# Seven-product steps in four chunk pairs of the second up product

## The chip, the cores and the metric

The kernel runs on one core of one Trainium2 chip. The metric is the device time of one execution in microseconds (us). Engines: TensorE (PE, its weight loads PEld), VectorE (DVE), ScalarE (ACT), GpSimd (POOL) and SyncE (SP).

## The reference

Two transformer-like blocks in float32 on 256 tokens of width 2048. The part that the change touches is the gated feed-forward product of the second block:

```
h = rmsnorm_2(x, g_ffn)                       # 256 x 2048
u = causal_dwconv(h @ w_up, ffn_conv_w) + ffn_conv_b   # w_up 2048 x 11264, conv of width 3 over tokens
gate, val = split(u, 2)
x = x + (silu(gate) * val) @ w_down
```

## The kernel before

**Numbers.** Every float32 operand is split in two fp32r numbers, hi and lo. A product is three matmuls, hi by hi, hi by lo and lo by hi. The activations are TensorE's weights (128x128), the weight matrix streams through as 128x512.

**Granules.** A weight matrix arrives in granules of 128x1024: two k tiles of 512 columns. SP loads a granule into one of four raw slots (L868), once the granule four before it has been split. ScalarE casts it to `wh` (L937), VectorE makes the remainder `wl` (L1293), TensorE multiplies it with `multiply_half` (L1868): two k tiles, two halves of the tokens, three matmuls, 12 in all. `wh` and `wl` have four slots (RING), so a cast waits until TensorE has left the granule four before it (L936). A chunk is 512 output columns, here 8 granules, and sums into two PSUM banks.

**Order.** Everything is planned in steps, one a granule: in step s granule s is cast and split, granule s-3 is multiplied, and small work is put down at chosen steps with `later`. Within a step stand first the granule, then the small work in the order in which it was put down. Each engine then goes through its part of the plan strictly in this order, and waits at semaphores in front of each operation. So an operation whose input is late holds up all that stands behind it on its engine.

**The second up product** (`w_up2`, operand `ffn2`, tiles `x4g`): 22 chunks. The first two are interleaved, the others follow each other. What follows a chunk that ends at granule L is planned by `plan_up` from s = L + 4: `up_rows` (ScalarE, PSUM to ST, L1215) at s, `turn` (VectorE transposes ST into Y, L1410, L1412) and `leave` (POOL stores Y to HBM, L1816) at s+1, `bring` (POOL loads it back, rearranged, into Z, four transfers, L1824) at s+3, `up_keep` (ScalarE, Z to FW, L1223) at s+9, then the convolution's taps: `up_first` at s+10 (ScalarE, four, L1231), `up_second` at s+11 (VectorE, four, L1740), `up_third` at s+12 (VectorE, four, L1747, L1750), `up_silu` at s+13 (ScalarE, L1235), `up_gated` (VectorE, L1754) and `act2_hi` (ScalarE, L1239) at s+14, `act2_lo` (VectorE, L1758) at s+15.

**The seven-product step** is there already in the gated stage (the up product of the first block, ten pairs of chunks) and in both down products. Two chunks of a pair are multiplied side by side. For chosen rows p of the weight (a row is two k tiles) the two granules of row p, one of each chunk, are taken together as a 2x2 product of blocks (two halves of tokens or k by two chunks) and computed with seven block products of three matmuls, 21 instead of 24. For it VectorE adds weight blocks (`sums`, three operations, L1321, L1324, L1326), ScalarE casts three blocks (`base_hi`, L957) and the four sums (`forms_hi`, L963), VectorE makes the remainders (`base_lo`, L1307; `forms_lo`, L1330). TensorE multiplies in two parts, `multiply_base` (9 matmuls) and `multiply_forms` (12). Four of the products gather in four shared PSUM banks. Five steps behind a pair's last such row `shared_out` copies them out (ScalarE, four, L979), then `shared_sums` (L1366, L1368), `shared_last` (L1373, L1375) and per chunk `shared_bank` (L1396, L1397, L1401) add them up and into the chunks' own banks on VectorE. Once a stage the sums of activation blocks are made (`xs_sum`, `xs_hi`, `xs_lo`). Fetches of a step's successor four granules on wait for its `base_lo`.

Of the kernel before, what the change touches and what calls it, by code (L numbers as in the profile page):

```python
# [8 lines left out]
P = 128  # L9
# [11 lines left out]
ALU = mybir.AluOpType  # L21
ACT = mybir.ActivationFunctionType
F32 = mybir.dt.float32
# [74 lines left out]
def two_block_kernel(nc, t, out):  # L98
    with ExitStack() as ctx:
# [10 lines left out]
        def view(name, shape, offset, dt=F32):  # L110
            return nc.alloc_sbuf_tensor_at(name, shape, dt, offset=offset)
# [115 lines left out]
        tile_sums = tmp.rearrange("p (k c) -> p k c", k=4)  # L227
# [4 lines left out]
        xs_in, gated_in = (view(n, [P, 2, 4, P], o) for n, o in (("xs_in", o_a), ("gated_in", o_b + 32 * K)))  # L232
        xs_out, gated_out = (view(n, [P, 2, 4, P], o) for n, o in (("xs_out", o_a + 4 * K), ("gated_out", o_b + 36 * K)))
# [44 lines left out]
        seven_operand = {"gated": "ffn", "out1": "act1", "down": "act2"}  # L278
        side_by_side = {"gated": {}, "out1": {}, "down": {}}
# [68 lines left out]
        def turn(step, src, filled):  # L348
# [133 lines left out]
        def plan_gated(n):  # L482
            def after(s, chunk):
                chunk.drained = [("silu", n), ("gated", n)]
                if n // 2 in GATED_PAIRS:
                    do("shared_bank", n)
# [12 lines left out]
            return after  # L499
# [178 lines left out]
        for n in range(2, 22):  # L678
            last_up = product(t["w_up2"], "N", "ffn2", PAIRS16, ("up", n), plan_up(n), n)
# [79 lines left out]
        def gated_at(n):  # L759

            return at("shared_bank", n) if n // 2 in GATED_PAIRS else product_of("gated", n)
# [54 lines left out]
        bases = {"gated": (gated_hi, gated_lo), "out1": (base_hi, base_lo), "down": (base_hi, base_lo)}  # L816
        x_places = {"gated": (gated_in, gated_out), "out1": (xs_in, xs_out), "down": (xs_in, xs_out)}
# [4 lines left out]
        def x_forms(unit):  # L822

            if unit.pair.stage == "gated":
                return [[x[:, unit.place, n] for x in (gated_xs_hi, gated_xs_lo)] for n in range(4)]
            k = 2 * unit.p
            return [[x[:, k, P:T] for x in operands[seven_operand[unit.pair.stage]]]] + [
                [x[:, unit.place, n] for x in (xs_hi, xs_lo)] for n in range(3)]
# [87 lines left out]
        def scalar(e):  # L916
# [8 lines left out]
            for name, args in phases:  # L925
# [32 lines left out]
                elif name == "forms_hi":  # L958
# [3 lines left out]
                    e.wait_ge(*at("sums", i))  # L962
                    e.copy(two_slots(wh, i), tile_sums.rearrange("p k c -> p (k c)")).then_inc(done[name], 1)  # L963
                elif name == "xs_hi":
                    stage, j = args
                    e.wait_ge(*at("xs_sum", stage, j))
                    if stage == "gated":
                        e.copy(gated_xs_hi[:], gated_out[:]).then_inc(done[name], 1)
                        continue
                    e.copy(seven_tiles(operands[seven_operand[stage]][0], stage, j)[:, :, 1], xs_out[:, :, 0])  # L970
                    e.copy(xs_hi[:, 2 * j:2 * j + 2], xs_out[:, :, 1:4]).then_inc(done[name], 1)
                elif name == "shared_out":
# [5 lines left out]
                    for k, place in enumerate((0, 3, 2, 1)):  # L978
                        e.copy(tile_sums[:, place, :], ps[:, pair.shared + k, :]).then_inc(done[name], 1)  # L979
# [228 lines left out]
                elif name == "up_rows":  # L1208
# [5 lines left out]
                    e.wait_ge(*product_of("up", n))  # L1214
# [49 lines left out]
        def vector(e):  # L1264
# [22 lines left out]
            for name, args in phases:  # L1287
# [20 lines left out]
                elif name == "sums":  # L1308
                    i, = args
                    unit = seven[i]  # L1310
                    b12, b11, b22, b21 = (two_slots(raw, i)[:, 512 * k:512 * k + 512] for k in range(4))
                    if unit is not unit.pair.units[0]:
                        e.wait_ge(*at("forms_lo", unit.former.i))
                    else:
# [12 lines left out]
                elif name == "forms_lo":  # L1327
                    i, = args
                    e.wait_ge(*at("forms_hi", i))
                    e.tensor_tensor(two_slots(wl, i), tile_sums.rearrange("p k c -> p (k c)"), two_slots(wh, i).bitcast(F32),  # L1330
                                    ALU.subtract).then_inc(done[name], 1)
                elif name == "xs_sum":
# [3 lines left out]
                    if j > 0:  # L1336
                        e.wait_ge(*at("xs_lo", stage, j - 1))
                    elif stage != "gated":

                        e.wait_ge(*through(last_ffn if stage == "out1" else last_up))  # L1340
# [9 lines left out]
                elif name == "xs_lo":  # L1350
                    stage, j = args
                    e.wait_ge(*at("xs_hi", stage, j))
                    if stage == "gated":
                        e.tensor_tensor(gated_xs_lo[:], gated_out[:], gated_xs_hi[:].bitcast(F32),
                                        ALU.subtract).then_inc(done[name], 1)
                        continue
                    hi, lo = (seven_tiles(x, stage, j)[:, :, 1] for x in operands[seven_operand[stage]])
# [3 lines left out]
                elif name == "shared_sums":  # L1361

                    stage, q = args
                    p1, p7, p6, _ = (tile_sums[:, k, :] for k in range(4))
# [4 lines left out]
                elif name == "shared_last":  # L1369
                    stage, q = args  # L1370
                    _, second, first, p5 = (tile_sums[:, k, :] for k in range(4))
# [4 lines left out]
                elif name == "shared_first":  # L1376
# [5 lines left out]
                    e.tensor_tensor(X[:, 0, n0], X[:, 0, n0], tile_sums[:, 0, :], ALU.add)  # L1382
                    e.tensor_tensor(X[:, 1, n0], X[:, 1, n0], tile_sums[:, 1, :], ALU.subtract).then_inc(done[name], 1)
                elif name == "shared_second":
# [4 lines left out]
                    e.tensor_tensor(X[:, :, n1], X[:, :, n1], tile_sums[:, 2:4, :], ALU.add).then_inc(done[name], 1)  # L1389
                elif name == "shared_bank":  # L1390
                    n, = args
                    bank0, bank1 = banks(named["gated", n])
                    e.wait_ge(*product_of("gated", n))
                    if n % 2 == 0:
                        e.wait_ge(*at("shared_sums", "gated", n // 2))
                        e.tensor_tensor(bank0, bank0, tile_sums[:, 0, :], ALU.add)  # L1396
                        e.tensor_tensor(bank1, bank1, tile_sums[:, 1, :], ALU.subtract).then_inc(done[name], 1)  # L1397
                    else:
                        b = named["gated", n].bank
                        e.wait_ge(*at("shared_last", "gated", n // 2))  # L1400
                        e.tensor_tensor(ps[:, b:b + 2, :], ps[:, b:b + 2, :], tile_sums[:, 2:4, :], ALU.add).then_inc(done[name], 1)  # L1401
# [774 lines left out]
```

## Time and profile before

| | us |
|---|---|
| median of 3 runs (2407.12 to 2408.91) | 2408.24 |
| the profiled execution | 2406.19 |
| its span | 2404.4 |
| TensorE busy | 2391.4 (99%) |
| VectorE busy | 1748.8 (73%) |
| ScalarE busy | 1351.3 (56%) |

Busy time is the sum of an engine's operations. Matmuls are pipelined: each lasts 0.389 us in the records and they start closer than that, so a busy share of 99% says only that one or another was always under way. The second up product lies between 1686.24 and 2164.96 us from the span's start.

### The profile page before, as it was taken

The numbers are of one execution on the slowest core, as the hardware profiler recorded it, in microseconds if no ns is written. First come the engines' busy times: TensorE is split into PE (matmuls) and PEld (weight loads), VectorE is DVE, ScalarE is ACT, GpSimd is POOL, SyncE is SP. The second block draws the span as 40 slices with busy tenths as digits, with TensorE's granted clock in tenths as the row PEclk, the third lists the DMA queues.
The fourth block names the chain that finished last, engine by engine and source line by source line (L and its number), as shares of the span: only waits on it lengthen the run. The fifth ranks groups of instructions, "written<-read, shape, count | busy, mean of one in ns | idle before, by whom it ended". The sixth has DMA issues, their size and how long they took to land.

```text
span 2404.4 us, 28031 instructions
## 1 busy us (share of the span) xinstructions
PE 2391.4 (99%) x10606; PEld 1980.6 (82%) x10606; DVE 1748.8 (73%) x2148; ACT 1351.3 (56%) x1649; POOL 190.6 (8%) x351
## 2 busy tenths in 40 slices
PE   9999999999999999999999999999999999999998
PEld 7888888888888887888888888888888888888887
DVE  7575555666778888888787865786577766678886
ACT  7554565445555555555555754544566666665554
POOL 0000000001000000000001100111111111110000
PEclk9999999999999999999999999999999999999999
DMA  8777656678866776776678877888788888887664
GB/s 275 225 222 231 195 189 184 216 237 248 257 218 218 230 224 212 227 253 220 195 227 274 249 233 220 257 243 236 237 241 250 242 243 242 241 241 206 220 214 160
DMA packets 155734, 550.06 MB, mean 229 GB/s; under 512 B 20176, under 2 KB 20688, under 8 KB 155216
## 3 DMA queue, kind: packets, MB, share of 16 engines
q1 hardware_dynamic: 131552, 470.91, 62.4%
q0 software_dynamic: 23472, 76.57, 11.7%
q8 instruction: 84, 1.38, 0.2%
q10 hardware_dynamic: 576, 0.79, 0.1%
q14 instruction: 50, 0.41, 0.1%
HBM read 507.82 MB, written 40.37 MB: 228 GB/s over the span
## 4 chain that ended last, share of the span: by engine, by line
PE 94%; DVE 3%; DMA 1%; ACT 1%; issue 1%; SPq 0%; ACTq 0%; DVEq 0%
PE ps L1868 93%; DMA raw<-in_w_ffn_in 1%; DVE wl L1293 1%; DMA raw<-in_w_in 0%; DVE tmp L1321 0%; ACT wh L937 0%; DVE wl L1330 0%; ACT wh L963 0%; ACT tmp L979 0%; DVE gated_lo L1307 0%; DVE tmp L1324 0%; DVE tmp L1326 0%; PE ps L2006 0%; PE ps L2026 0%; DVE ps L1401 0%
## 5 line engine op out<-in xcount | busy, mean ns | idle before, releaser
L1293 DVE TENSOR_TENSOR wl<-raw,wh 128x1024 fp32r<-128x1024 f32 x786 | 954.3, 1221 | 589.2 <-ACT wh L937 588.0
L937 ACT CAST wh<-raw 128x1024 fp32r<-128x1024 f32 x786 | 821.1, 1050 | 739.5 <-PE ps L1868 709.6
L1868 PE MATMUL ps<-wh,x4g_lo 128*128 128x512 f32 x704 | 273.9, 389 | 0.0
L1868 PE MATMUL ps<-wh,x4g_hi 128*128 128x512 f32 x704 | 273.9, 389 | 0.0
L1868 PE MATMUL ps<-wl,x4g_hi 128*128 128x512 f32 x704 | 273.9, 389 | 0.0
L1868 PE MATMUL ps<-wh,h_hi 128*128 128x512 f32 x576 | 224.4, 392 | 2.3 <-DVE wl L1293 1.3
L1868 PE MATMUL ps<-wh,h_lo 128*128 128x512 f32 x576 | 223.0, 389 | 0.0
L1868 PE MATMUL ps<-wl,h_hi 128*128 128x512 f32 x576 | 222.8, 389 | 0.0
L1868 PE MATMUL ps<-wh,x1g_lo 128*128 128x512 f32 x564 | 219.4, 389 | 0.0
L1868 PE MATMUL ps<-wl,x1g_hi 128*128 128x512 f32 x564 | 219.4, 389 | 0.0
L1868 PE MATMUL ps<-wh,x1g_hi 128*128 128x512 f32 x564 | 219.4, 389 | 0.0
L1868 PE MATMUL ps<-wh,act_hi 128*128 128x512 f32 x560 | 217.9, 389 | 0.0
L1868 PE MATMUL ps<-wl,act_hi 128*128 128x512 f32 x560 | 217.8, 389 | 0.0
L1868 PE MATMUL ps<-wh,act_lo 128*128 128x512 f32 x560 | 217.8, 389 | 0.0
L1824 POOL DMA_DIRECT2D Z<-rows x268 | 146.2, 552 | 337.0 <-DMA rows<-Y 324.1
L1816 POOL DMA_DIRECT2D rows<-Y x67 | 37.6, 561 | 1622.4 <-DVE Y L1412 1622.4
L1868 PEld LDWEIGHTS ps<-wl,x4g_hi 128*128 128x128 f32 x704 | 132.1, 188 | 27.6
L1868 PEld LDWEIGHTS ps<-wh,x4g_lo 128*128 128x128 f32 x704 | 132.1, 188 | 27.4
L1868 PEld LDWEIGHTS ps<-wh,x4g_hi 128*128 128x128 f32 x704 | 132.1, 188 | 27.4
L963 ACT CAST wh<-tmp 128x2048 fp32r<-128x2048 f32 x44 | 84.3, 1915 | 90.5 <-DVE tmp L1326 85.5
L1868 PEld LDWEIGHTS ps<-wh,h_hi 128*128 128x128 f32 x576 | 108.0, 188 | 25.0 <-issue 2.0
L1868 PEld LDWEIGHTS ps<-wh,h_lo 128*128 128x128 f32 x576 | 108.1, 188 | 22.7
(380 smaller groups left out, 4065.4 us busy)
## 6 DMA issues: line engine op xcount, KB each, us to landing
raw<-in_w_in SPq DMA_DIRECT2D x196, 512.0 KB, 4.3
raw<-in_w_ffn_in SPq DMA_DIRECT2D x176, 512.0 KB, 4.3
raw<-in_w_up SPq DMA_DIRECT2D x176, 512.0 KB, 4.6
raw<-in_w_ffn_out SPq DMA_DIRECT2D x88, 512.0 KB, 4.2
raw<-in_w_down SPq DMA_DIRECT2D x88, 512.0 KB, 4.3
rows<-Y POOLq DMA_DIRECT2D x67, 512.0 KB, 5.1
Z<-rows POOLq DMA_DIRECT2D x268, 128.0 KB, 4.9
raw<-in_w_o SPq DMA_DIRECT2D x32, 512.0 KB, 4.7
```

The source lines that it names most:

```text
L937: e.copy(wh[:, i % RING, :], raw[:, slot, :]).then_inc(rounded, 1)
L963: e.copy(two_slots(wh, i), tile_sums.rearrange("p k c -> p (k c)")).then_inc(done[name], 1)
L1293: e.tensor_tensor(wl[:, r, :], raw[:, i % RAW, :], wh[:, r, :].bitcast(F32), ALU.subtract).then_inc(remainder, 1)
L1816: e.dma_start(rows_out[n % 2], Y[:]).then_inc(rows_left[n % 2], 16)
L1824: e.dma_start(ZA[32 * q:32 * q + 32], rows_out[n % 2, :, 256 * q:256 * q + 256].rearrange("(a i) e -> i a e", a=4)).then_inc(rows_back[n % ...
L1868: return e.matmul(dst, weights, x, start=start, stop=stop, skip_group_check=True)
```

## The change

Pairs 1, 3, 5 and 7 of the second up product (chunks 2 and 3, 6 and 7, 10 and 11, 14 and 15) are multiplied side by side, with rows 4 and 6 as seven-product steps, at the third and fifth place of the order 0, 1, 4, 2, 6; rows 3, 5 and 7 follow chunk by chunk. The pair's chunks gather in banks 4 to 7 and the shared products in banks 0 to 3. Bases, sums of activations and the tile sums get places of their own in SBUF (`up_sums` instead of `tmp`). The chunks behind a pair wait for its `shared_out`. `up_late(n)` gives for each chunk by how many steps its rows, its bring and its taps are put off. The first down pair waits for rows 14 and 15 where it waited for earlier work. The weight is stored in the host's arrays with the blocks of the chosen rows exchanged.

```diff
-SEVEN = {"gated": (4, 6), "out1": (8, 10, 12, 14, 16, 18), "down": (8, 10, 12, 14, 16, 18)}
+SEVEN = {"gated": (4, 6), "up": (4, 6), "out1": (8, 10, 12, 14, 16, 18), "down": (8, 10, 12, 14, 16, 18)}
+UP_PAIRS = (1, 3, 5, 7)
+UP_ORDER = (0, 1, 4, 2, 6, 3, 5, 7)
...
-            later(step + 2, lambda: do("bring", n))
+            later(step + 2 + late, lambda: do("bring", n))
...
+        def up_late(n):
+            if n < 2:
+                return ((0, 0, 2), (1, 6, 6))[n]
+            if n // 2 in UP_PAIRS:
+                return (1, 0, 0) if n % 2 == 0 else (4, 0, 0)
+            next_sums = n // 2 + 1 in UP_PAIRS
+            if n // 2 - 1 in UP_PAIRS and n % 2 == 0:
+                return 2, 0, 6 * next_sums
+            return 0, 7 * next_sums, 7 * next_sums
...
-                s += (0, 4, 2)[n] if n < 3 else 0
+                rows_late, bring_late, take_late = up_late(n)
+                if n // 2 in UP_PAIRS:
+                    later(s + n % 2 * 2, lambda: do("shared_bank", "up", n))
+                s += rows_late
...
-                    rows_of["up", n] = turn(s + 1, ST, ("up_rows", n))
+                    rows_of["up", n] = turn(s + 1, ST, ("up_rows", n), bring_late)
...
+                s += take_late
                 later(s + 9, take)
...
-        for n in range(2, 22):
-            last_up = product(t["w_up2"], "N", "ffn2", PAIRS16, ("up", n), plan_up(n), n)
+        plan_x_sums("up", len(granules), 0)
+        for q in range(1, 11):
+            if q in UP_PAIRS:
+                cleared = [[("pool_out", 1)], [("x_split", 1, 1)]] if q == 1 else [[("up_rows", 2 * q - 4 + n)] for n in range(2)]
+                product_side_by_side(t["w_up2"], "up", q, 4, UP_ORDER, 5, [plan_up(2 * q), plan_up(2 * q + 1)], 0, cleared,
+                                     ("shared_out", "shared_sums", "shared_last"))
+                continue
+            for n in (2 * q, 2 * q + 1):
+                last_up = product(t["w_up2"], "N", "ffn2", PAIRS16, ("up", n), plan_up(n), n)
+                if q - 1 in UP_PAIRS:
+                    last_up.cleared = [("shared_out", "up", q - 1)]
...
-            cleared = ([("pool_out", 1)], [("x_split", 1, 1)]) if q == 0 else ([("shared_out", "down", 0)],) * 2
+            cleared = ([("up_rows", 14)], [("up_rows", 15)]) if q == 0 else ([("shared_out", "down", 0)],) * 2
```

With the steps counted from the first granule of a pair behind two plain chunks C and D, the plan of the small work is: of the former pair's second chunk up_keep 0, up_first 1, up_second 2, up_third 3, silu 4, gated and act2_hi 5, act2_lo 6; D's up_rows 3 and turn 4; the first seven-product step 5 (granules 4 and 5), the second 9 (granules 8 and 9); C's up_keep 12, up_first 13, up_second 14, up_third 15, silu 16, gated and act2_hi 17, act2_lo 18; shared_out 13, shared_sums 14, shared_last 15; shared_bank of the pair's chunks 16 and 21, their up_rows 17 and 23, turns 18 and 24; D's bring 13, up_keep 19, taps 20 to 25.

## Rows read from the trace of the kernel before

**Rows 1.** the page: busy times by engine, and the chain that ended last by line.

```profile
PE 2391.4 (99%) x10606; PEld 1980.6 (82%) x10606; DVE 1748.8 (73%) x2148; ACT 1351.3 (56%) x1649; POOL 190.6 (8%) x351
...
PE ps L1868 93%; DMA raw<-in_w_ffn_in 1%; DVE wl L1293 1%; DMA raw<-in_w_in 0%; DVE tmp L1321 0%; ACT wh L937 0%; DVE wl L1330 0%; ACT wh L963 0%; ACT tmp L979 0%; DVE gated_lo L1307 0%; DVE tmp L1324 0%; DVE tmp L1326 0%; PE ps L2006 0%; PE ps L2026 0%; DVE ps L1401 0%
```

**Rows 2.** timeline, TensorE in up; start, duration, engine, line, operation, operands.

```profile
1814.08 0.39 PE L1868 MATMUL ps<-wh,x4g_hi 128*128 128x512 f32 x1
...
1816.80 0.39 PE L1868 MATMUL ps<-wh,x4g_hi 128*128 128x512 f32 x1
```

**Rows 3.** windows of up, up and gated: us; PE, PEld, DVE, ACT, POOL busy; clock, DMA.

```profile
1686.24:2164.96 478.72, 478.72 (x2113) 396.40 (x2112) 330.53 (x443) 297.29 (x393) 60.27 (x110) 1.00 0.83 242
1773.30:1816.80 43.50, 43.50 (x193) 36.02 (x192) 33.02 (x50) 28.12 (x38) 5.47 (x10) 1.00 0.85 248
800.00:842.20 42.20, 42.20 (x187) 34.90 (x187) 36.00 (x37) 23.21 (x27) 2.74 (x5) 1.00 0.71 223
```

**Rows 4.** groups of the gated stage: busy, mean ns, idle before and its releaser.

```profile
L1868 PE MATMUL ps<-wh,gated_xs_hi 128*128 128x512 f32 x60 | 23.7, 395 | 0.7 <-DVE wl L1330 0.7
...
L1868 PE MATMUL ps<-gated_hi,x1g_hi 128*128 128x512 f32 x40 | 15.7, 393 | 1.0 <-DVE gated_lo L1307 1.0
```

**Rows 5.** timeline, ScalarE in the second up product.

```profile
1800.85 0.62 ACT L1223 COPY FW<-Z 128x512 f32<-128x512 f32 x1
...
1801.89 1.05 ACT L937 CAST wh<-raw 128x1024 fp32r<-128x1024 f32 x1
1802.85 2.08 ACT L1231 ACTIVATE tmp<-FW,cst 128x256 f32<-128x256 f32 x4
...
1811.45 0.64 ACT L1235 ACTIVATE tmp<-tmp 128x512 f32<-128x512 f32 x1 [1.50 <-DVE tmp L1750]
...
1814.92 0.62 ACT L1239 CAST act_hi<-tmp 128x512 fp32r<-128x512 f32 x1 [1.89 <-DVE tmp L1754]
...
1817.06 1.05 ACT L937 CAST wh<-raw 128x1024 fp32r<-128x1024 f32 x1 [0.56 <-PE ps L1868]
1818.01 0.68 ACT L1215 ACTIVATE tmp<-ps,small 128x512 f32<-128x512 f32 x1
```

**Rows 6.** timeline, VectorE in the second up product.

```profile
1802.74 0.70 DVE L1410 STREAM_TRANSPOSE Y<-tmp 128x512 f32<-128x512 f32 x1
...
1807.05 1.66 DVE L1740 SCALAR_TENSOR_TENSOR tmp<-FW,cst,tmp 128x255 f32<-128x255 f32 x4
1808.62 1.22 DVE L1293 TENSOR_TENSOR wl<-raw,wh 128x1024 fp32r<-128x1024 f32 x1
1809.76 1.26 DVE L1747 SCALAR_TENSOR_TENSOR tmp<-FW,cst,tmp 128x254 f32<-128x254 f32 x3
...
1814.20 0.68 DVE L1754 TENSOR_TENSOR tmp<-tmp 128x512 f32<-128x512 f32 x1
```

**Rows 7.** timeline, VectorE in a gated pair.

```profile
913.03 1.22 DVE L1321 TENSOR_TENSOR tmp<-raw 128x1024 f32<-128x1024 f32 x1 [3.02 <-DMA raw<-in_w_ffn_in]
...
915.62 1.75 DVE L1307 TENSOR_TENSOR gated_lo<-raw,gated_hi 128x1536 fp32r<-128x1536 f32 x1
917.75 2.29 DVE L1330 TENSOR_TENSOR wl<-tmp,wh 128x2048 fp32r<-128x2048 f32 x1 [0.38 <-ACT wh L963]
...
929.28 0.69 DVE L1366 TENSOR_TENSOR tmp<-tmp 128x512 f32<-128x512 f32 x1
...
935.41 0.69 DVE L1396 TENSOR_TENSOR ps<-ps,tmp 128x512 f32<-128x512 f32 x1
```

**Rows 8.** timeline, ScalarE in the same gated pair.

```profile
915.81 1.90 ACT L963 CAST wh<-tmp 128x2048 fp32r<-128x2048 f32 x1 [1.35 <-DVE tmp L1326]
...
925.12 2.03 ACT L979 COPY tmp<-ps 128x512 f32<-128x512 f32 x4
```

**Rows 9.** timeline, TensorE at that pair's second step.

```profile
917.52 0.47 PE L1868 MATMUL ps<-gated_hi,x1g_hi 128*128 128x512 f32 x1 [0.52 <-DVE gated_lo L1307]
```

**Rows 10.** window of that pair, columns as in group 3.

```profile
906.60:948.80 42.20, 41.43 (x181) 33.63 (x180) 34.85 (x37) 22.14 (x25) 1.41 (x4) 1.00 0.72 222
```

More of the change, by code:

```diff
@@ L226, in two_block_kernel @@
         gated_lo = view("gated_lo", [P, 3, 512], o_x + 6 * K, FR)
-        tile_sums = tmp.rearrange("p (k c) -> p k c", k=4)
+        up_hi = view("up_hi", [P, 3, 512], o_b + 28 * K, FR)
+        up_lo = view("up_lo", [P, 3, 512], o_b + 74 * K, FR)
+        up_sums = view("up_sums", [P, 4, 512], o_b + 80 * K)
+        up_xs_hi = view("up_xs_hi", [P, 2, 4, P], o_b + 34 * K, FR)
+        up_xs_lo = [view(f"up_xs_lo{i}", [P, 4, P], o_b + at * K, FR) for i, at in enumerate((38, 72))]
+        tile_sums_of = {stage: up_sums if stage == "up" else tmp.rearrange("p (k c) -> p k c", k=4)
+                        for stage in ("gated", "out1", "up", "down")}
         xs_hi = view("xs_hi", [P, 6, 3, P], o_a + 12 * K, FR)
@@ L346, in product_side_by_side, with turn @@
                 later(chunk.last + RING + late, lambda s=chunk.last + RING + late, n=n: afters[n](s, pair.chunks[n]))
-        def turn(step, src, filled):
+        def turn(step, src, filled, late=0):
             n = len(turns)
@@ L485, in after @@
                 if n // 2 in GATED_PAIRS:
-                    do("shared_bank", n)
+                    do("shared_bank", "gated", n)
                     later(s + 1, lambda: do("silu", n))
@@ L759, in gated_at, with up_at @@
         def gated_at(n):
-            return at("shared_bank", n) if n // 2 in GATED_PAIRS else product_of("gated", n)
+            return at("shared_bank", "gated", n) if n // 2 in GATED_PAIRS else product_of("gated", n)
+        def up_at(n):
+            return at("shared_bank", "up", n) if n // 2 in UP_PAIRS else product_of("up", n)
         def product_of(*key):
@@ L814, in two_slots @@
             return x[:, i % RING:i % RING + 2, :].rearrange("p r c -> p (r c)")
[L816 to L817 removed]
+        bases = {"gated": (gated_hi, gated_lo), "out1": (base_hi, base_lo), "up": (up_hi, up_lo),
+                 "down": (base_hi, base_lo)}
+        x_places = {"gated": (gated_in, gated_out), "out1": (xs_in, xs_out), "up": (up_in, up_out),
+                    "down": (xs_in, xs_out)}
         def all_three(x):
@@ L825, in x_forms @@
                 return [[x[:, unit.place, n] for x in (gated_xs_hi, gated_xs_lo)] for n in range(4)]
+            if unit.pair.stage == "up":
+                return [[x[:, n] for x in (up_xs_hi[:, unit.place], up_xs_lo[unit.place])] for n in range(4)]
             k = 2 * unit.p
@@ L962, in scalar @@
                     e.wait_ge(*at("sums", i))
+                    tile_sums = tile_sums_of[seven[i].pair.stage]
                     e.copy(two_slots(wh, i), tile_sums.rearrange("p k c -> p (k c)")).then_inc(done[name], 1)
@@ L966, in scalar @@
                     e.wait_ge(*at("xs_sum", stage, j))
-                    if stage == "gated":
-                        e.copy(gated_xs_hi[:], gated_out[:]).then_inc(done[name], 1)
+                    if stage in ("gated", "up"):
+                        x_hi = gated_xs_hi if stage == "gated" else up_xs_hi
+                        e.copy(x_hi[:], x_places[stage][1][:]).then_inc(done[name], 1)
                         continue
@@ L978, in scalar @@
                     for k, place in enumerate((0, 3, 2, 1)):
-                        e.copy(tile_sums[:, place, :], ps[:, pair.shared + k, :]).then_inc(done[name], 1)
+                        e.copy(tile_sums_of[stage][:, place, :], ps[:, pair.shared + k, :]).then_inc(done[name], 1)
                 elif name == "first_hi":
@@ L1310, in vector @@
                     unit = seven[i]
+                    tile_sums = tile_sums_of[unit.pair.stage]
                     b12, b11, b22, b21 = (two_slots(raw, i)[:, 512 * k:512 * k + 512] for k in range(4))
@@ L1313, in vector @@
                         e.wait_ge(*at("forms_lo", unit.former.i))
+                    elif unit.pair.stage == "up":
+                        if unit.pair.q > UP_PAIRS[0]:
+                            e.wait_ge(*at("shared_bank", "up", 2 * unit.pair.q - 3))
                     else:
@@ L1329, in vector @@
                     e.wait_ge(*at("forms_hi", i))
+                    tile_sums = tile_sums_of[seven[i].pair.stage]
                     e.tensor_tensor(two_slots(wl, i), tile_sums.rearrange("p k c -> p (k c)"), two_slots(wh, i).bitcast(F32),
@@ L1363, in vector @@
                     stage, q = args
-                    p1, p7, p6, _ = (tile_sums[:, k, :] for k in range(4))
+                    p1, p7, p6, _ = (tile_sums_of[stage][:, k, :] for k in range(4))
                     e.wait_ge(*at("shared_out", stage, q))
@@ L1370, in vector @@
                     stage, q = args
-                    _, second, first, p5 = (tile_sums[:, k, :] for k in range(4))
+                    _, second, first, p5 = (tile_sums_of[stage][:, k, :] for k in range(4))
                     e.wait_ge(*at("shared_sums", stage, q))
@@ L1398, in vector @@
                     else:
-                        b = named["gated", n].bank
-                        e.wait_ge(*at("shared_last", "gated", n // 2))
+                        b = named[stage, n].bank
+                        e.wait_ge(*at("shared_last", stage, n // 2))
                         e.tensor_tensor(ps[:, b:b + 2, :], ps[:, b:b + 2, :], tile_sums[:, 2:4, :], ALU.add).then_inc(done[name], 1)
```

36 lines of the change are left out of this document (23 added, 13 removed).

## The prediction

> **What bounds the kernel now.** I read the page first: TensorE is busy for 2391 of 2404 us and line 1868 holds 93% of the chain that ended last [rows 1]. Busy matmuls can hide spacing, so I then read their starts: in the second up product the first matmul of a weight granule starts at 1814.08 and that of the next at 1816.80, that is 12 matmuls in 2.72 us, 0.2267 us each [rows 2]. The windows by stage show no hole there: 478.72 us busy of 478.72. Over 43.50 us (two chunks) VectorE works 33.0 and ScalarE 28.1 us; in a 42.2 us pair with two seven-product steps of the gated stage VectorE works 36.0 and ScalarE 23.2 [rows 3]. The gated stage is the model of the change. It runs nearly without loss, but not quite: its matmuls wait 1.0 us for the base remainders and 0.7 us for the remainders of the sums [rows 4]. So TensorE binds, and the question is whether VectorE and ScalarE, which work strictly in a written order, still hand over each granule in time.
>
> **What the change removes.** A seven-product step does with 21 matmuls what two granules do with 24. Eight such steps save 24 x 0.2267 = 5.44 us on the path that sets the end.
>
> The Trainium skill, "TensorE: Matmul & The Clock Gate", Back-to-back issue gap, gives N/2.4 + 2.5 ns for an isolated matmul, 215.8 ns at 512 columns, which would make the saving 5.18 us. The trace has 226.7 ns.
>
> **What it adds.** Durations are read as start to next start where operations follow without idle. ScalarE: cast of a granule 0.96, up_keep 1.04, four taps up_first 1.99 (2.08 less the seam), silu 0.54, act2_hi 0.53, up_rows 1.17 (two of 0.68 less their seams) [rows 5]. Its cast starts 0.26 after the start of the next granule's matmuls (1817.06 against 1816.80) [rows 2, 5]. VectorE: remainder of a granule 1.14 in a row, 1.22 to its end, four up_second 1.58, up_third the same, gated 0.68 to its end, turn 1.22 [rows 6]. A seven-product step: sums 2.59, base_lo 1.67 to 1.75, forms_lo 2.21 to 2.29; shared_sums 1.33 (two of 0.69 with the handover between them, less the seam), shared_last as much, shared_bank 1.20 (two of 0.69) [rows 7]. On ScalarE forms_hi 1.90 and the four copies of shared_out 1.90 [rows 8]. Per pair VectorE gets 2 x 6.5 for four remainders of 1.14, and 2 x 1.33 + 1.20 + about 1.14, together some 13 us more. A pair and the two plain chunks behind it then give VectorE 28 remainders (31.9), two steps (13.0), 5.0 for the shared sums and four times 5.6 for turn and taps: some 72 of the 85.7 us that they take on TensorE, enough on average. What decides is the order, so I lay out one pair. Zero is the start of its first granule g0 on TensorE; TensorE starts U1 (in place of g4, g5) at 10.88, g6 at 15.64, U2 (for g8, g9) at 21.08, g10 at 25.84, then one granule each 2.72, the first of the next plain chunk, g16, at 42.16. A granule can be cast when TensorE has left the one four before it.
>
> *Tail, all four pairs.* The planner puts the taps of the chunk in front (C) on steps 12 to 18: up_keep at 12, up_first at 13, up_second at 14, up_third at 15, silu at 16, gated and act2_hi at 17. On 13, 14 and 15 stand also shared_out, shared_sums and shared_last, on 16 shared_bank and on 17 up_rows of the pair's first chunk. ScalarE may cast g12 at 26.10, when U2 is multiplied, and then has no idle: cast 0.96, up_keep 1.04, cast 0.96, shared_out 1.90, up_first 1.99, so g14 is cast at 32.95 to 34.0. VectorE starts at 34.03 and has g14 1.14, shared_sums 1.33, up_second 1.58, g15 (done 39.30, wanted 39.39), shared_last 1.33, up_third 1.58, g16 1.22: done at 43.35, wanted at 42.1. TensorE stalls 1.24 and about 0.1 for its restart, 1.35 us. Then VectorE has shared_bank 1.20, g17 1.14, gated 0.68 (46.3); only then ScalarE does act2_hi 0.53, up_rows 1.17 and the cast of g18 1.05, and VectorE its remainder 1.22, done at 50.3. Wanted, with the stall before it, at 48.9: 1.54 us. With act2_lo, the turn and g19 another 0.25 follow. Together 3.1 us. From step 20 on the queues catch up; the taps of the second plain chunk, at 19 to 25, come out 0.5 us ahead at the tightest.
>
> *Head, pairs two to four.* Steps 0 to 6 carry the taps of the second chunk of the former pair. ScalarE casts g0 at -7.15 behind an act2_hi, then up_keep, g1, up_first and g2, to -1.15. VectorE has g2 from -1.12, up_second, g3, up_third and the turn to 5.54, then U1: sums 8.2, base_lo 9.9, forms_lo 12.55, wanted at 12.87, in time. Behind it come gated to 13.15, act2_hi on ScalarE, the cast of g6 to 14.8, its remainder to 16.0; wanted 15.59: 0.55 us with the restart. act2_lo and g7 hold VectorE until 17.7, so U2's sums end at 20.35 and base_lo at 22.0, wanted at 21.5 (0.62), and forms_lo at 24.7, wanted at 24.2 (0.56). Together 1.7 us. Before the first pair no such taps lie; the operand sums (six VectorE operations once) lie there instead, and I count it as nothing, at most the 1.7 of the others.
>
> *Transfers.* SP fetches g8 and g9 only once U1's base_lo is done. In a gated pair this step waited for the landing (the idle of 3.02 us before 913.03) [rows 7], and here, issued at 9.9, it has 7.8 us until VectorE is free for U2 at 17.7. It is just covered. bring_late of 7 steps keeps the row transfers of the chunk in front out of this stretch, on POOL's queue, where nothing else waits behind them. An unlucky landing adds up to 1 us a pair.
>
> *Everything else at nothing.* The sums have a buffer of their own, so no wait on the rows or taps is added; up_xs and the cleared banks of the down product wait for work that ended many steps earlier.
>
> **The sum.** -5.44 + 4 x 3.1 + 3 x 1.7 = +12.1 us. The profiled execution took 2406.19; 2418.3 for it, and as the median of the runs is 2.05 above, 2420.3 us. Lower bound of the unknown: the handovers cost as little as in the gated stage (1.7 us for ten pairs in the groups shown), -5.44 + 0.7 = -4.7. Upper bound: each pair also loses 1 us to landings and the head costs 1.7 in pair one too, +17.8.
>
> The Trainium skill, "Perfetto Trace Analysis", Identifying the Most-Contended Engine, says to improve the engine with the highest occupancy and takes occupancy as a fair measure for Vector and Scalar. By that, 72 of 85.7 us on VectorE leave room, and the change gains its 5 us; the trace agrees only in part: at 36.0 of 42.2 us the gated stage already has short waits [rows 3, 4].
>
> **Rivals.** (A) The layout by hand, slower by 12 us: 0.70, own range 2414 to 2426. For it: each link is a measured duration in program order, and the chain from g12's cast to g16's remainder has no slack in it. Against it: it takes every handshake of some 20 operations as fixed; 0.05 us less in each would take a third of the loss.
> (B) The average decides: the queues absorb the bursts as in the gated stage, 2403 to 2404 us: 0.12. For it: no stall in up now and 85% load. Against it: gated has no up_first and turns rows once per pair.
> (C) The first tail stall comes (VectorE's rate from g14 to g16), but the chain over act2_hi and up_rows and the head find room: -5.44 + 4 x 1.35 = 0, 2408 us: 0.10. The point of decision is whether up_rows runs before act2_hi's wait ends.
> (D) The landing of g8 and g9 binds: 2425 to 2431 us: 0.06. For it the 3.02 us; against it VectorE is late anyhow.
> (E) TensorE's granted clock falls from 2.4 GHz in the stalls: 0.02. The wait of 0.52 us before 917.52 left the granted clock of that pair's window at 1.00 [rows 9, 10]; one granule at the lower level of 1.2 GHz would cost 2.7 us more, so one behind each of the four tails 11 us above A.
>
> **Chances and range.** The likeliest is A: 2420.3. B and C reach below 2409; with C in and B and the upper part of D out the range is 2407 to 2427. Faster by over 0.2% (4.8 us, about what a measurement here can tell) needs nearly the whole saving: 0.09, most of B. Within 0.2%: the rest of B, and C, 0.13. Slower: 0.78.
>
> **What would show it.** In the profile after: TensorE 24 matmuls fewer in the stage and idle before them, released by VectorE's wl, at four places where the plain chunk behind a pair begins (1.3 us) and two granules later (1.5 us); three times smaller idle before g6 and before both halves of U2. ScalarE without idle from g12's cast to g14's. If no TensorE idle appears in the stage, the layout is wrong and B holds. If the idle before U2 is released by a transfer, D does. If the first tail stall stands alone, C does.

## The result, and the profile after

| | before | after |
|---|---|---|
| median, us (5 runs each) | 2407.12 (2405.27 to 2408.91) | 2474.27 (2469.61 to 2474.97) |
| span of the profiled execution, us | 2404.4 | 2472.5 |
| second up product, us | 478.72 | 545.59 |
| its matmuls | 2112 | 2088 |
| its time above 0.2267 us a matmul | 0 | 72.3 |

The changed kernel is slower, ratio 1.0273 [1.0261 to 1.0285]. 2420.3 with a range to 2427 was forecast, so the direction was right, and more than five times the loss came. All but about 1 us of it lies in the second up product: 72.3 - 5.44 = +66.9 us; the stage begins 0.9 us later, and the down product behind it is as long as before.

The page of the changed kernel answers to [rows 1]. Busy time by engine, the chain that ended last by engine and by line, and a group of matmuls:

```profile
PE 2408.5 (97%) x10582; PEld 1983.5 (80%) x10582; DVE 1801.8 (73%) x2206; ACT 1360.9 (55%) x1666; POOL 190.6 (8%) x351
...
PE 78%; DVE 11%; DMA 4%; ACT 4%; issue 2%; POOL 0%; SPq 0%; ACTq 0%; DVEq 0%; POOLq 0%
...
L1927 PE MATMUL ps<-wh,x4g_hi 128*128 128x512 f32 x648 | 258.2, 398 | 44.0 <-DVE wl L1338 43.9
```

VectorE's share is 73% as before, and the idle of TensorE is put down to it. The windows of the same kernel, to be held against [rows 3]: the two first chunks; pair one; the two plain chunks behind it with the next pair's start.

```profile
1687.20:1729.80 42.60, 42.60 (x190) 35.27 (x188) 28.21 (x45) 23.45 (x32) 2.75 (x5) 1.00 0.77 226
1729.80:1772.00 42.20, 42.20 (x188) 34.86 (x187) 33.20 (x36) 25.33 (x29) 3.32 (x6) 1.00 0.69 216
1772.00:1834.00 62.00, 50.91 (x211) 40.76 (x210) 39.22 (x54) 34.68 (x50) 8.20 (x15) 0.92 0.68 207
```

Pair one itself costs nothing. The loss stands behind it, where also the granted clock drops to 0.92. TensorE there, matmuls without idle between left out:

```profile
1772.66 0.39 PE L1927 MATMUL ps<-wh,x4g_lo 128*128 128x512 f32 x1
1774.16 0.47 PE L1927 MATMUL ps<-wh,x4g_hi 128*128 128x512 f32 x1 [1.12 <-DVE wl L1338]
...
1779.50 0.39 PE L1927 MATMUL ps<-wh,x4g_lo 128*128 128x512 f32 x1
1781.02 0.50 PE L1927 MATMUL ps<-wh,x4g_hi 128*128 128x512 f32 x1 [1.13 <-DVE wl L1338]
...
1786.56 0.39 PE L1927 MATMUL ps<-wh,x4g_lo 128*128 128x512 f32 x1
1795.79 0.80 PE L1927 MATMUL ps<-wh,x4g_hi 128*128 128x512 f32 x1 [8.84 <-DVE wl L1338]
1796.38 0.63 PE L1927 MATMUL ps<-wl,x4g_hi 128*128 128x512 f32 x1
1796.81 0.63 PE L1927 MATMUL ps<-wh,x4g_lo 128*128 128x512 f32 x1
```

The first two gaps are the forecast ones: in front of g16 and of g18 (the first and third granule of the plain chunk), 1.40 and 1.43 us with their restart. The third, in front of g20, was in no forecast: 9.23 us, and behind it ten matmuls, from 1796.38 on, follow at 0.427 us instead of 0.227; the granted clock over them is 0.50, which is the lower level of 1.2 GHz. Here is the chain that ended last through this place: start, duration, what.

```profile
1781.56 0.62 DVE Y L1469
1782.18 0.60 DVE Y L1471
...
1783.34 0.56 POOL rows L1875
1783.90 1.62 POOL Z L1883 x3
1785.51 6.80 DMA Z<-rows
...
1792.39 0.06 ACT FW L1268
```

It is not VectorE. VectorE transposes the rows of the pair's first chunk (Y), POOL stores them (`rows`, L1875), POOL fetches rows into Z (L1883), they land, and only then can ScalarE do `up_keep` (FW from Z, L1268). The rows fetched are those of D, the second chunk in front of the pair, whose own store was long done. ScalarE's timeline shows what was queued behind the wait, the cast of the next granule:

```profile
1778.66 1.99 ACT L980 CAST wh<-raw 128x1024 fp32r<-128x1024 f32 x2
1792.39 0.62 ACT L1268 COPY FW<-Z 128x512 f32<-128x512 f32 x1 [11.75 <-DMA Z<-rows]
1792.92 0.61 ACT L1269 COPY FW<-Z 128x512 f32<-128x512 f32 x1
1793.44 1.04 ACT L980 CAST wh<-raw 128x1024 fp32r<-128x1024 f32 x1
```

The waits of the stage confirm that this comes four times, once behind each pair (engine, line, waited for, us in total, times, longest):

```profile
ACT FW L1268 <- DMA Z<-rows: 46.1, 4, 11.7
PE ps L1927 <- DVE wl L1338: 43.9, 13, 8.8
PE ps L1927 <- DVE up_lo L1352: 6.5, 4, 3.0
```

Why POOL asks so late stands in the code. The diff leaves `leave` reading `s` when it runs, and by then the new line `s += take_late` has been carried out. So the bring of D goes to 3 + 3 + 7 + 7 = step 20 of the pair, not to step 13, where the plan above lists it: behind the store of the pair's first chunk (`leave` at step 18) in POOL's queue, and one step behind the `up_keep` at 19 that needs it. (In front of pair one, whose trace stands above, the numbers are 4 + 3 + 6 + 6 = 19, the step of that `up_keep` itself.)

Where the 72.3 us are, summed from the starts of the matmuls:

| place | forecast | measured |
|---|---|---|
| tails (g16, g18, g19), four pairs | 12.4 | 12.1 |
| g20 behind each pair | 0 | 43.8 |
| heads of pairs two to four, up to the last granule of the pair | 5.1 | 4.75 + 4.05 + 6.08 = 14.9 |
| elsewhere in the plain chunks | 0 | 1.5 |

### The profile page after: what moved, and what is told of

The parts are those of the page before. It is cut to its first block, busy times and chain, and to the rows that moved or that the text cites. A ratio compares the mean times of both kernels' runs of the same rounds, so it can differ in the third digit from the quotient of the medians.

```text
span 2472.5 us, 28091 instructions
## 1 busy us (share of the span) xinstructions
PE 2408.5 (97%) x10582; PEld 1983.5 (80%) x10582; DVE 1801.8 (73%) x2206; ACT 1360.9 (55%) x1666; POOL 190.6 (8%) x351
## 3 DMA queue, kind: packets, MB, share of 16 engines
q0 software_dynamic: 23472, 76.57, 11.3%
## 4 chain that ended last, share of the span: by engine, by line
PE 78%; DVE 11%; DMA 4%; ACT 4%; issue 2%; POOL 0%; SPq 0%; ACTq 0%; DVEq 0%; POOLq 0%
PE ps L1927 77%; DVE wl L1338 3%; ACT wh L980 1%; DMA raw<-in_w_ffn_in 1%; DMA raw<-in_w_up 1%; DMA Z<-rows 1%; DVE wl L1380 1%; ACT tmp L1276 1%; DVE tmp L1799 1%; ACT wh L1007 1%; DMA raw<-in_w_in 1%; DVE tmp L1806 0%; DVE tmp L1370 0%; DMA raw<-in_w_ffn_out 0%; ACT up_sums L1024 0%
## 5 line engine op out<-in xcount | busy, mean ns | idle before, releaser
L1338 DVE TENSOR_TENSOR wl<-raw,wh 128x1024 fp32r<-128x1024 f32 x770 | 933.8, 1220 | 600.1 <-ACT wh L980 598.8
L980 ACT CAST wh<-raw 128x1024 fp32r<-128x1024 f32 x770 | 798.7, 1049 | 646.4 <-PE ps L1927 607.9
L1927 PE MATMUL ps<-wh,x4g_hi 128*128 128x512 f32 x648 | 258.2, 398 | 44.0 <-DVE wl L1338 43.9
L1927 PE MATMUL ps<-wl,x4g_hi 128*128 128x512 f32 x648 | 255.8, 395 | 0.0
L1927 PE MATMUL ps<-wh,x4g_lo 128*128 128x512 f32 x648 | 255.4, 394 | 0.0
L1927 PEld LDWEIGHTS ps<-wh,x4g_hi 128*128 128x128 f32 x648 | 124.0, 191 | 77.6 <-DVE wl L1338 45.7
L1875 POOL DMA_DIRECT2D rows<-Y x67 | 37.5, 560 | 1735.2 <-DVE Y L1471 1735.2
L1883 POOL DMA_DIRECT2D Z<-rows x268 | 146.3, 552 | 290.6 <-DMA rows<-Y 243.1
L1927 PEld LDWEIGHTS ps<-wh,x4g_lo 128*128 128x128 f32 x648 | 123.8, 191 | 26.4
L1927 PEld LDWEIGHTS ps<-wl,x4g_hi 128*128 128x128 f32 x648 | 123.9, 191 | 25.2
L1007 ACT CAST wh<-tmp 128x2048 fp32r<-128x2048 f32 x44 | 84.3, 1915 | 90.9 <-DVE tmp L1375 88.9
```

What stands on the lines that cost most here:

```text
L980: e.copy(wh[:, i % RING, :], raw[:, slot, :]).then_inc(rounded, 1)
L1338: e.tensor_tensor(wl[:, r, :], raw[:, i % RAW, :], wh[:, r, :].bitcast(F32), ALU.subtract).then_inc(remainder, 1)
L1875: e.dma_start(rows_out[n % 2], Y[:]).then_inc(rows_left[n % 2], 16)
L1883: e.dma_start(ZA[32 * q:32 * q + 32], rows_out[n % 2, :, 256 * q:256 * q + 256].rearrange("(a i) e -> i a e", a=4)).then_inc(rows_back[n % ...
L1927: return e.matmul(dst, weights, x, start=start, stop=stop, skip_group_check=True)
```

## The experiments

All are timed against the kernel before on the same chip, 4 to 12 runs each; its median lay between 2405.72 and 2407.32 us. "Excess" is the time of the up product above 0.2267 us a matmul, as in the table; the saving of 5.44 us goes off it.

**The bring in front of the wait.** The changed kernel with the variable bound early:

```diff
-                def leave():
+                def leave(s=s):
```

> The changed kernel with one word more: leave() keeps the step s that it had when it was put down, so a chunk's bring is no longer moved a second time by take_late and stands at step 13, in front of the copy (step 19) that waits for it. Theory 1 (the long stall is that copy waiting for a transfer that POOL may only issue behind the next rows' store): the four stalls of 9 us before granule g4 behind a pair and the matmuls at 1.2 GHz behind them go, the two stalls of 1.3 us in front of them stay; 8 to 14 us above before, about 2419. Rival 1 (the stall is contention of transfers while the seven-product steps fetch, wherever bring stands): still over 30 us above before. Rival 2 (ScalarE and VectorE are overloaded in the pairs): the 9 us move to another granule, over 30 us above before as well.

Measured 2429.0 us, ratio 1.0096 [1.0083 to 1.0110]; excess 25.6. 45 us of the loss are gone. POOL's timeline, first of the changed kernel, then of this one:

```profile
1744.57 0.55 POOL L1875 DMA_DIRECT2D rows<-Y  x1 [8.71 <-DVE Y L1471]
1745.11 2.21 POOL L1883 DMA_DIRECT2D Z<-rows  x4
1783.34 0.56 POOL L1875 DMA_DIRECT2D rows<-Y  x1 [36.01 <-DVE Y L1471]
1783.89 2.18 POOL L1883 DMA_DIRECT2D Z<-rows  x4
```

```profile
1741.10 2.19 POOL L1883 DMA_DIRECT2D Z<-rows  x4 [3.61 <-DMA rows<-Y]
1746.19 0.56 POOL L1875 DMA_DIRECT2D rows<-Y  x1 [2.91 <-DVE Y L1471]
1761.88 2.18 POOL L1883 DMA_DIRECT2D Z<-rows  x4 [15.13 <-ACT FW L1269]
1786.04 0.56 POOL L1875 DMA_DIRECT2D rows<-Y  x1 [21.98 <-DVE Y L1471]
```

In the second D's rows are fetched at 1761.88, 24 us ahead of the store at 1786.04, and ScalarE reads them without a wait. The tails stay at 3.00 to 3.03 us each, as the layout has them (3.1). The heads cost 1.1, 4.6, 3.9 and 3.9 us. That, and a stage that began 2.6 us later than in the kernel before, is what lies above what I expected. C's bring moves too (from step 6 back to 0, in pair one from 6 to 4); the next experiment leaves it late.

**The bring by its number.** The changed kernel, closure as it is, with no lateness asked for D's bring, so that it falls on step 13 as well:

```diff
-                return ((0, 0, 2), (1, 6, 6))[n]
+                return ((0, 0, 2), (1, 0, 6))[n]
...
-            return 0, 7 * next_sums, 7 * next_sums
+            return 0, 0, 7 * next_sums
```

> The changed kernel with its closure as it is, but bring_late 0 instead of 7 and 6 for the chunks whose taps are put off, so that D's bring again comes to stand at step 13, by a number instead of by the binding. C's bring stays at step 6, where the changed kernel has it. Theory 1: as e1 within 3 us, about 2429. If the binding did something else as well (rows or turns at other steps), it stays near the changed kernel.

Measured 2426.24 us, ratio 1.0079 [1.0064 to 1.0095], tails 3.03 again. Two different edits with the same place of D's bring give nearly the same time; that place is the cause, and C's bring is not.

**The late bring alone.** The kernel before, without any seven-product step in up, with the row transfers of chunks 5, 9, 13 and 17 seven steps later:

```diff
-                    rows_of["up", n] = turn(s + 1, ST, ("up_rows", n))
+                    rows_of["up", n] = turn(s + 1, ST, ("up_rows", n), 7 if n in (5, 9, 13, 17) else 0)
```

> The kernel before, without any seven-product step, with one thing of the change: the bring of chunks 5, 9, 13 and 17 stands 7 steps later, one step behind the copy that waits for it and behind the next chunk's store. Theory 1: four stalls of some 9 us minus the slack of the plain stage (about 4 us), each followed by slow matmuls if it is long enough: 20 to 50 us above before. Rivals 1 and 2 (contention or load of the seven-product steps): within 5 us of before, since all that they blame is absent.

Measured 2426.92 us, ratio 1.0088 [1.0074 to 1.0101]; four stalls of 3.6 to 5.0 us, excess 18.4. A wait of its list, and POOL at one of the four places:

```profile
ACT FW L1223 <- DMA Z<-rows: 37.9, 4, 9.6
```

```profile
1936.38 0.55 POOL L1816 DMA_DIRECT2D rows<-Y  x1 [21.20 <-DVE Y L1412]
1936.92 2.21 POOL L1824 DMA_DIRECT2D Z<-rows  x4
```

The late transfer does it without the rest of the change. ScalarE waits nearly as long (9.5 us each), but gaps of 3.4 to 3.7 us reach TensorE; presumably the casts are further ahead without a tail.

**Nothing put off.** The first experiment's kernel, the lateness of C's and D's taps and of D's row transfers taken out (here and below, `s=s` of the first experiment stays in and isn't shown again):

```diff
-                return ((0, 0, 2), (1, 6, 6))[n]
+                return ((0, 0, 0), (1, 3, 3))[n]
...
-            next_sums = n // 2 + 1 in UP_PAIRS
-            if n // 2 - 1 in UP_PAIRS and n % 2 == 0:
-                return 2, 0, 6 * next_sums
-            return 0, 7 * next_sums, 7 * next_sums
+            return (2, 0, 0) if n // 2 - 1 in UP_PAIRS and n % 2 == 0 else (0, 0, 0)
```

> The seven-product steps as in the changed kernel, bring in front of its copy, but the taps of the two chunks in front of a pair not put off (chunk C's copy at step 6 instead of 12, chunk D's at 12 instead of 19). Theory 1 with the layout by hand: C's taps then stand around the second step (8 and 9), D's around shared_out (13) to up_rows (17); stalls of 3 to 6 us a pair, 5 to 18 us above before. Rival (putting off is what costs, the steps themselves are hidden): 2402 to 2406.

Measured 2434.31 us, ratio 1.0121 [1.0105 to 1.0136]: excess 32.7, 20.7 of it within pairs two to four. So putting the taps off is worth 5 us by the medians and 7 by the excess; it is the transfer put off with them that costs.

**The rows in front of act2_hi.** The first experiment's kernel, with `up_rows` of a pair's first chunk as the first action of its step:

```diff
-                later(s, lambda: do("up_rows", n))
+                if n // 2 in UP_PAIRS and n % 2 == 0:
+                    todo.setdefault(s, []).insert(0, lambda: do("up_rows", n))
+                else:
+                    later(s, lambda: do("up_rows", n))
```

> As e1, but in step 17 ScalarE does the up_rows of the pair's first chunk in front of C's act2_hi, which waits for VectorE. Tests one link of the layout by hand. If the stall of 1.5 us before g2 behind a pair is that chain (shared_bank, g17, gated, act2_hi, up_rows, cast, remainder), it falls to 0.4 or less in all four pairs, and the rest stays: about 4.5 us under e1. Rival (it is VectorE's total load there): no change from e1 within 1 us, the 1.5 us moved to g3 or g4.

Measured 2424.27 us, ratio 1.0071 [1.0057 to 1.0084]: the stall before g18 fell from 1.46 to 0.27 to 0.35 us in all four pairs. ScalarE, first of the first experiment, then of this one (whose lines stand three lower):

```profile
1779.68 0.62 ACT L1284 CAST act_hi<-tmp 128x512 fp32r<-128x512 f32 x1 [2.50 <-DVE tmp L1813]
1780.21 0.68 ACT L1260 ACTIVATE tmp<-ps,small 128x512 f32<-128x512 f32 x1
```

```profile
1776.43 0.69 ACT L1263 ACTIVATE tmp<-ps,small 128x512 f32<-128x512 f32 x1 [0.86 <-DVE ps L1459]
1777.02 0.68 ACT L1264 ACTIVATE tmp<-ps,small 128x512 f32<-128x512 f32 x1
1778.08 0.62 ACT L1287 CAST act_hi<-tmp 128x512 fp32r<-128x512 f32 x1 [0.37 <-DVE tmp L1816]
```

The rows ran in the 2.50 us in which ScalarE had waited for the gated result. That link of the forecast's chain is shown, and it is worth 4.7 us.

**Planned again.** The first experiment's kernel with tap times 1 to 2 steps nearer, the pair's own included:

```diff
-                return ((0, 0, 2), (1, 6, 6))[n]
+                return ((0, 0, 0), (1, 6, 5))[n]
...
-                return (1, 0, 0) if n % 2 == 0 else (4, 0, 0)
+                return (1, 0, -2) if n % 2 == 0 else (4, 0, -2)
...
-                return 2, 0, 6 * next_sums
-            return 0, 7 * next_sums, 7 * next_sums
+                return 2, 0, 4 * next_sums
+            return 0, 7 * next_sums, 6 * next_sums
```

> As e1, and the taps spread by hand over the steps in which VectorE has idle time: C's copy at step 10 instead of 12 (taps before shared_out), D's at 18, the pair's own two chunks 2 steps earlier (24 and 30). Theory 1 with the layout by hand: the chain from g12's cast to g16's remainder loses one copy and four taps, the head loses the taps before g6; stalls under 1 us a pair, so 2402 to 2406. Rival 2 (overload): no order helps, as e1 within 3 us.

Measured 2424.84 us, ratio 1.0076 [1.0063 to 1.0088]. No stall is left at g16 to g19; in the two plain chunks behind three of the pairs 0.5 to 0.8 us are lost, 2.1 behind the fourth. But the first step of the next pairs now waits 3.6 to 5.2 us: what no longer delays the tail comes out at the head, where D's rows now end 8.7 us behind the start of g0, against 3.1 to 3.8 in the first experiment.

**Spread by lag.** Due times chosen over both at once; `shared_last` 2 steps and the second `shared_bank` 1 step later as well:

```diff
-                return ((0, 0, 2), (1, 6, 6))[n]
+                return ((2, 0, -2), (1, 2, 4))[n]
...
-                return (1, 0, 0) if n % 2 == 0 else (4, 0, 0)
+                return (1, 0, -1) if n % 2 == 0 else (4, 0, -1)
...
-                return 2, 0, 6 * next_sums
-            return 0, 7 * next_sums, 7 * next_sums
+                return 1, 0, 4 * next_sums
+            return 2 * next_sums, 0, 3 * next_sums
```

> As e1, with the small work of the four chunks laid anew: C's rows one step sooner and its copy at step 9, D's rows at 5 and its copy at 17, the pair's own copies at 25 and 31, shared_last two steps and the second shared_bank one step later. e4 showed that the lag of VectorE and ScalarE is carried into the next pair (3.6 to 5.2 us lost at its first step), so this layout follows the queues through a whole period, not one pair. Theory 1 (only the order loses time, the steps themselves fit): under 1 us of stall a pair, and the whole saving of 5.4 us shows less what landings cost: 2400 to 2404, faster than before. Rival (a period has too much work for VectorE or too many transfers): 2410 to 2425 as e4.

Measured 2405.24 us, ratio 0.9995 [0.9986 to 1.0004]: level with before. The tails are empty, and 4.69 us are left before the first step of pairs two to four (1.7, 0.7, 2.3). In pair four, VectorE at `sums`, then ScalarE, then TensorE:

```profile
1994.31 0.69 DVE L1813 TENSOR_TENSOR tmp<-tmp 128x512 f32<-128x512 f32 x1
1995.81 1.23 DVE L1370 TENSOR_TENSOR up_sums<-raw 128x1024 f32<-128x1024 f32 x1 [0.81 <-DMA raw<-in_w_up]
```

```profile
1998.60 1.91 ACT L1007 CAST wh<-up_sums 128x2048 fp32r<-128x2048 f32 x1 [1.36 <-DVE up_sums L1375]
2000.41 0.68 ACT L1260 ACTIVATE tmp<-ps,small 128x512 f32<-128x512 f32 x1
2000.99 0.68 ACT L1261 ACTIVATE tmp<-ps,small 128x512 f32<-128x512 f32 x1
```

```profile
2001.76 0.47 PE L1927 MATMUL ps<-up_hi,x4g_hi 128*128 128x512 f32 x1 [2.01 <-ACT tmp L1261]
```

`sums` waits for a landing, 1.29 us in pair two, nothing in pair three and 0.81 us in pair four. But what releases TensorE in all three is `up_rows` of D (L1260, L1261), which empties the banks of the shared products. This layout put it at step 5, so on ScalarE it stands behind `forms_hi` (L1007), which waits for `sums`. TensorE starts 0.10 us behind the end of these rows each time, and the bases had been ready 1.5 us before that end. The four experiments that follow were aimed at the landing alone.

**As fourth and fifth row.** The spread layout with order 0, 1, 2, 4, 6 and due times to fit.

> The kernel of the spread layout, but the two seven-product steps stand as fourth and fifth row of a pair instead of third and fifth, the last granules behind them; the remaining due times are moved to fit (rows of C 1 step late, its row transfers 4 and its taps 3; D's row transfers and taps 6 and 6; in the pair rows 1 and 5 late, taps 1 earlier; shared sums 1 step and shared_last 2 steps later, second bank at +4). What was left of TensorE idle in the spread layout, 4.69 us, stood before the first seven-product step, whose fetch landed 6.7 us after its issue. Theory (the landing is what is left): one row more in front of the first step gives its fetch up to 5.4 us more, 1 to 2 us of idle are left, and the kernel takes before - 5.44 + 1.5, some 2402 to 2404 (2402.5). Rival (VectorE is what is left): the two steps follow each other at once and ask 13.0 us of VectorE while TensorE works 9.5 us on them; then 2 to 3 us of idle per pair stand before the second step, -5.44 + 4 x 2.5 = +4.6, some 2411.

Measured 2409.87 us, ratio 1.0012 [1.0004 to 1.0021]. The rival's mechanism, smaller than it said: 1.3 to 2.7 us a pair around the second step, 6.8 in all.

**Three with C's rows one step earlier.** The first of them against the spread layout:

```diff
-                return ((2, 0, -2), (1, 2, 4))[n]
+                return ((1, 0, -1), (1, 5, 4))[n]
...
-                return (1, 0, -1) if n % 2 == 0 else (4, 0, -1)
+                return (1, 1, -1) if n % 2 == 0 else (4, 0, -1)
...
-                return 1, 0, 4 * next_sums
-            return 2 * next_sums, 0, 3 * next_sums
+                return 0, 8 * next_sums, 4 * next_sums
+            return 2 * next_sums, 4 * next_sums, 3 * next_sums
```

> The kernel of the spread layout with third and fifth row kept; the row transfers of C come 8 steps later, those of D 4 steps later (with their taps 4 and 5 steps later in all), the ones of the pair's first chunk 1 step later. In the spread layout the fetch for the first seven-product step was issued at 1988.995 while row transfers issued at 1986.61 were under way. Theory (that collision makes the 4.69 us that are left): with the transfers elsewhere 1 to 2 us are left, 2402 to 2404. Rival (any fetch takes as long at this place, with or without row transfers beside it): 4 to 5 us of idle are left and the time is that of the spread layout and of the kernel before, 2405 to 2407. I hold the rival for as likely.

Measured 2401.47 us (11 runs, 2398.45 to 2404.76; before 2406.47), ratio 0.9975 [0.9967 to 0.9984], the fastest kernel of this study: 5.0 us less than before. Its window over the up product, and VectorE at the same `sums`:

```profile
1689.50:2162.70 473.20, 473.20 (x2089) 391.98 (x2088) 383.44 (x501) 311.90 (x410) 60.31 (x110) 1.00 0.81 245
```

```profile
1992.77 0.68 DVE L1813 TENSOR_TENSOR tmp<-tmp 128x512 f32<-128x512 f32 x1
1993.37 1.21 DVE L1370 TENSOR_TENSOR up_sums<-raw 128x1024 f32<-128x1024 f32 x1
```

The excess is 0: the stage takes 2088 x 0.2267 = 473.28 us. But my theory named the row transfers, and the next two take their lateness back, one each (`8 * next_sums` to 0 for C, `4 * next_sums` to 0 for D):

> The kernel with rows of C 8 late, one number changed: C's row transfers come at once again (8 steps back). Theory (that transfer's place is what took the last idle away): the waits for landings before the first seven-product step come back, 1 to 2 us of idle in each of pairs two to four, +3 to +5 us, 2405 to 2406, about the time of the spread layout. Rival (the other due times did it, or the run to run place of landings): within 0.1% of 2401.5. I give the theory 0.45.

> The kernel with rows of C 8 late, one number changed: D's row transfers come at once again (4 steps back), C's stay 8 late. Theory (D's row transfers met the fetch for the first seven-product step): idle before that step comes back, 1 to 2 us in pairs two to four, 2405 to 2406. Rival: no idle comes back, 2401.5, as its taps start late enough either way. I give the theory 0.4.

Measured 2402.55 and 2403.42 us, ratios 0.9980 [0.9971 to 0.9989] and 0.9979 [0.9971 to 0.9988], excess 0 in both. Both theories fell: neither transfer, put back alone, brings the idle back. Last, one number of those that all three share against the spread layout (they also share the due times around pair one, and the transfers of the pair's first chunk one step later):

```diff
-                return 1, 0, 4 * next_sums
+                return 0, 0, 4 * next_sums
```

> The kernel of the spread layout with one number changed: C's rows and everything of its taps one step earlier (rows at once instead of 1 late). This is what the three kernels without idle share against it, apart from the due times around pair one. Theory (that step decides): no idle or under 1 us in the stage, 2401.5 to 2403. Rival (the place of D's or C's row transfers or the pair's own matters together): idle stays before the first seven-product step, 2405 to 2407. I give the theory 0.6.

Measured 2402.27 us, ratio 0.9987 [0.9978 to 0.9997], excess 0.5 instead of 4.69. C's rows and taps one step earlier are enough. From the start of g0 on TensorE, VectorE now begins `sums` at 5.3, 3.7 and 3.6 us in pairs two to four, where the spread layout has 6.5, 5.5 and 7.1, and D's rows end at 11.2, 9.6 and 9.5 us instead of 12.4, 11.3 and 13.0; the first step is due at 10.88. So the wait that ended is the one for D's rows. Which of the moved instructions lets VectorE begin sooner was not taken apart; the landings explain 1.3, 0 and 0.6 us of it.

## Why the prediction was right in its direction and wrong in its size

*What bounds the kernel, and the saving.* Right. Without stalls the stage takes 473.28 us, 5.44 less than 478.72, in three kernels.

*The tail.* Right to a tenth: 3.03 us a pair against 3.1. VectorE in the changed kernel, from g14's remainder to g16's:

```profile
1764.71 1.23 DVE L1338 TENSOR_TENSOR wl<-raw,wh 128x1024 fp32r<-128x1024 f32 x1 [3.60 <-ACT wh L980]
...
1772.80 1.22 DVE L1338 TENSOR_TENSOR wl<-raw,wh 128x1024 fp32r<-128x1024 f32 x1
```

From 1764.71 to the end at 1774.02 are 9.31 us; the layout had 34.03 to 43.35. The idle of 3.60 us in front, a wait for ScalarE's cast, and the burst behind it are what the average over a pair doesn't show. So rival B is false for this layout, and C also: the second stall came in full, and the experiment with the rows in front of act2_hi shows that only the place of `up_rows` made it.

*The transfers: the step that failed.* "bring_late of 7 steps keeps the row transfers of the chunk in front out of this stretch, on POOL's queue, where nothing else waits behind them." I took the transfer to be late by `bring_late` alone. It is late by `bring_late` and `take_late`, step 20 (19 in pair one). I then asked only what waits behind the transfer, not what it waits behind (the store of the pair's first chunk, at 18) nor whether its reader (`up_keep`, at 19) comes first. Price: 4 x 11 = 43.8 us, of which some 9 each are idle and 2 the lower clock. With the two experiments on the bring's place and the one on the kernel before it is shown from both sides. The diff on the page held all of it.

*The heads.* g6 and the two halves of the second step were right where they appear (0.75, 0.62 and 0.60 in pair three, against 0.55, 0.62 and 0.56). "In time" was wrong for the first step: 1.5 to 4.9 us were lost before its base. "From step 20 on the queues catch up" is what failed: the layout has VectorE at the sums 5.54 us behind the start of g0, and with the bring in its place it got there at 7.7 to 8.4. The layout began each head from a rested state; that the tail's lag went through the two plain chunks into the next pair is how I read this. Removing the late bring did not remove this (2.0 and 1.4 us), the tail's relief made it larger (3.6 to 5.2), and only due times chosen for both ended it.

*The landing of g8 and g9 (D).* Not seen. In the spread layout the sums of the first step waited for a landing (1.29 and 0.81 us), but TensorE waited there for D's rows.

*The clock (E).* I gave it 0.02 since a wait of 0.52 us did nothing. It came, behind gaps some seventeen times as long, and so as a part of the failed step: some 2.3 us of each 11. It also took 1.7 and 2.9 us of the heads of pairs two and four, which the kernel with the bring in its place (granted clock 0.999) does not show.

*The sum.* Of the forecast's +12.1, the changed kernel with the bring in its place has +20.2 in this stage: tails 12.1, heads 13.6, saving 5.44. The range up to 2427 just misses it at 2429.0.

## What to carry to other kernels

When a change puts an action off, work out its final place in numbers, from the code as it runs (a closure reads its variable late), and hold it against two things on the same queue and on its reader's: what it now waits behind, and when the reader is due. One transfer behind the wrong store, once a pair, cost eight times the whole saving. And lay out the next period too: the heads were lost until tail and head were planned together; done so, the same change gave its full 5.4 us in its stage, and 3.7 to 5.0 us by the medians of the whole kernel. And when idle is left, read what releases the binding engine itself: VectorE's row named a landing, TensorE's row named ScalarE.

## What the runs showed of the hardware

What an idle TensorE costs beyond its idle was read from the starts behind each gap (start to start). Behind gaps of 1.5 us in the changed kernel, matmuls started 0.23 us apart again after the first. Behind the four of 8.5 to 9.2 us, 8 to 12 matmuls each (38 in all) came 0.427 us apart, at the lower granted clock. In between, the length alone did not decide: in the changed kernel 2.35 us in front of pair two's first step were followed by 7 such matmuls and 3.38 us in front of pair four's by 12, while 2.19 us at the same place with the bring moved in front were followed by none. With the late bring alone, 3.41 us were followed by none and three gaps of 3.5 to 3.6 us by 17 in all. The changed kernel's mean granted clock was 0.988 against 0.999.

Four transfers of 128 KB from HBM into Z took 8.5 us from POOL's first issue (1783.89) to ScalarE's read (1792.39), beside weight fetches. That is the time of three granules on TensorE (3 x 2.72 us), so at this place a reader less than that behind the issue waits.
